# Banded attention in items of two query blocks, in a one-core two-model transformer kernel

## The reference, cut to what matters

```python
    kb = band(k).astype(jnp.float32)          # block b of 128 queries sees the keys of blocks b-1 and b
    vb = band(v).astype(jnp.float32)
    s = jnp.einsum('bnjqhgd,bnjkhd->bnjhgqk', qb, kb) * scale
    ...
    s = jnp.where(mask[:, None, None, :, :], s, jnp.float32(NEG))
    m = jnp.max(s, axis=-1, keepdims=True)
    if sinks is not None:
        sk = sinks.astype(jnp.float32).reshape(Hkv, G)[:, :, None, None]
        m = jnp.maximum(m, sk)
        p = jnp.exp(s - m)
        denom = jnp.sum(p, axis=-1, keepdims=True) + jnp.exp(sk - m)
    ...
    o = jnp.einsum('bnjhgqk,bnjkhd->bnjqhgd', p / denom, vb)
```

## Time and profile before

| | us |
|---|---|
| median of 3 runs | 2407.29 |
| lowest, highest | 2406.37, 2409.31 |
| span of the profiled execution | 2406.4 |

### The profile page before, as it was taken

One profiled execution on the slowest core, in us unless ns is written; L12 is line 12 of the kernel. 1 busy time (PEld: TensorE's weight loads), 2 busy tenths in 40 slices (PEclk: granted clock), 3 DMA queues, 4 the chain that ended last, 5 costly groups with the idle time before them and its releaser, 6 DMA issues.

```text
span 2406.4 us, 29717 instructions
## 1 busy us (share of the span) xinstructions
PE 2379.8 (99%) x11108; PEld 1924.6 (80%) x11108; DVE 1209.2 (50%) x1961; ACT 965.8 (40%) x1513; POOL 1316.2 (55%) x1589
## 2 busy tenths in 40 slices
PE   8999999999999999999999999999999999999999
PEld 8777778888888888777787888888887777788887
DVE  5997765423224432379625743333325785266331
ACT  4554444322223223566524432332336764344321
POOL 5763246656556655366244765555554562466554
PEclk9999999999999999999999999999999999999999
DMA  5321123333333333222122333333332221223333
GB/s 166 109 71 53 47 77 97 96 97 97 97 97 110 97 97 103 71 72 69 54 87 79 97 97 97 96 97 97 97 98 67 72 78 53 88 87 98 96 97 96
DMA packets 59758, 213.40 MB, mean 89 GB/s; under 512 B 6624, under 2 KB 6752, under 8 KB 59488
## 3 DMA queue, kind: packets, MB, share of 16 engines
q1 hardware_dynamic: 59472, 211.38, 29.2%
q10 hardware_dynamic: 144, 0.14, 0.0%
HBM read 209.39 MB, written 2.10 MB: 88 GB/s over the span
## 4 chain that ended last, share of the span: by engine, by line
PE 91%; DVE 6%; issue 1%; ACT 1%; DMA 0%; POOL 0%; SPq 0%; DVEq 0%; ACTq 0%
PE banks L721 89%; DVE t L1203 1%; DVE t L1211 1%; DVE t L1213 1%; DVE t L1488 1%; DVE t L1204 1%; DVE t L1197 1%; DVE t L1219 0%; PE banks L841 0%; PE banks L995 0%; DVE t L1222 0%; ACT t L1679 0%; DMA t<-in_w 0%; PE banks L875 0%; POOL t L1992 0%
## 5 line engine op out<-in xcount | busy, mean ns | idle before, releaser
L721 PE MATMUL banks<-t,t 128*128 128x512 f32 (+4 forms) x10788 | 2351.7, 387 | 17.2 <-ACT t L1699 5.9
L721 PEld LDWEIGHTS banks<-t,t 128*128 128x128 f32 (+2 forms) x10788 | 1889.5, 188 | 452.2 <-issue 64.3
L1992 POOL TENSOR_TENSOR t<-t,t 128x256 fp32r<-128x256 f32 x1544 | 1258.9, 846 | 1049.9 <-ACT t L1679 1041.5
L1679 ACT ACTIVATE t<-t 128x1024 fp32r<-128x1024 f32 x385 | 408.2, 1060 | 1078.8 <-issue 605.5
L1197 DVE TENSOR_TENSOR t<-banks,t 128x512 f32<-128x512 f32 x121 | 83.1, 687 | 169.8 <-PE banks L721 169.2
L1378 DVE TENSOR_TENSOR t<-banks,t 128x512 f32<-128x512 f32 x44 | 30.4, 690 | 184.5 <-PE banks L721 184.3
L1346 DVE SCALAR_TENSOR_TENSOR t<-banks,t 128x512 f32<-128x512 f32 x32 | 22.1, 691 | 155.4 <-PE banks L721 155.4
L1080 DVE SCALAR_TENSOR_TENSOR t<-t,t,t 128x512 fp32r<-128x512 f32 x64 | 52.0, 817 | 58.1 <-ACT t L1699 58.1
L1323 DVE TENSOR_TENSOR t<-t,t 128x512 fp32r<-128x512 f32 x68 | 70.5, 1036 | 2.3
L1352 DVE TENSOR_TENSOR t<-banks,t 128x512 f32<-128x512 f32 x24 | 16.6, 691 | 106.0 <-PE banks L721 106.0
L1699 ACT ACTIVATE t<-t,t 128x512 fp32r<-128x512 f32 x64 | 45.6, 715 | 55.7 <-DVE t L1346 49.1
(11 more groups left out here) (182 smaller groups left out, 1304.7 us busy)
## 6 DMA issues: line engine op xcount, KB each, us to landing
t<-in_w SPq DMA_DIRECT2D x386, 512.0 KB, 3.5
t<-in_xT SPq DMA_DIRECT2D x8, 256.0 KB, 5.7
out<-t SPq DMA_DIRECT2D x8, 256.0 KB, 4.5
t<-in_dmask SPq DMA_DIRECT2D x1, 1536.0 KB, 7.7
t<-in_vbias SPq DMA_DIRECT2D x2, 384.0 KB, 4.1
t<-in_c SPq DMA_DIRECT2D x1, 576.0 KB, 8.6
t<-in_w SPq DMA_DIRECT2D x2, 256.0 KB, 3.9
t<-in_pos SPq DMA_DIRECT2D x2, 256.0 KB, 4.1
```

What stands on the lines that cost most here:

```text
L721: return pe.matmul(o, l, r, start=start, stop=stop, skip_group_check=True)
L1679: a.activation(whl[u % 2][:, 0:1024], wraw[u % 3][:, :], ACT.Copy).then_inc(*w_high.next(u))
L1992: p.tensor_tensor(hl[:, 1024:2048][:, c], wraw[u % 3][:, c], as_f32(hl[:, c]), ALU.subtract).then_inc(*w_low.next((u, q)))
```

## The change

An item (i, c) now takes query blocks 2c and 2c+1, so there are 8 items in place of 16. Each score bank holds both blocks of one head (512 columns). The mask tile is three blocks wide (first, other, other) and one slice of 512 serves both c; a second small DMA fills its third part. Transposes go into the two score banks, and the turned probabilities are copied over the probabilities themselves in one 1024-wide tile (`swa_S`). The negated maximum with the sink is one DVE operation per head pair half (`tensor_scalar` with max and mult), and exp(sink - max) is formed on ACT with the sink as bias. There are 8 transposes and 8 value matmuls in an item. The planner's rules and its list of items behind the heads are the same, with one item still behind each group until the eight are used.

```diff
-        swm_t = at(top[0], 512)
+        swm_t = at(top[0], 768)
...
+        swa_S = [reg(88 + 6 * s, 1024)[:, :] for s in range(3)]
+        swa_m = [small_t[:, 64 + 16 * s:80 + 16 * s] for s in range(3)]
...
-            def swa_scores(i, b):
+            def swa_scores(i, c):
...
+                for q in range(2):
+                    b = 2 * c + q
+                    k0 = 128 * max(b - 1, 0)
+                    for hf in range(2):
+                        rows = slice(64 * hf, 64 * hf + 64)
+                        ins = mm(B[bk[hf]][:, 256 * q:256 * q + 256], QB[i][rows, 128 * b:128 * b + 128],
+                                 KBt[rows, k0:k0 + 256])
...
-                for k in range(4):
-                    ins = pe.transpose(B[bb][:, 128 * k:128 * k + 128], reg_S[slot][0][:, 128 * k:128 * k + 128], C["ident"])
...
+                for hf in range(2):
+                    for k in range(4):
+                        ins = pe.transpose(B[bk[hf]][:, 128 * k:128 * k + 128],
+                                           swa_S[slot][:, 512 * hf + 128 * k:512 * hf + 128 * k + 128], C["ident"])
...
+            def swa_soft(i, c):
...
                 for hf in range(2):
-                    v.scalar_tensor_tensor(out=sx[:, 256 * hf:256 * hf + 256], in0=B[pair(slot)[hf]][:, 0:256],
-                                           scalar=0.125, in1=mk, op0=M_, op1=A_).then_inc(*v_attn.next())
+                    v.scalar_tensor_tensor(out=sx[:, 512 * hf:512 * hf + 512], in0=B[pair(slot)[hf]], scalar=0.125,
+                                           in1=swm_t[:, 256 * c:256 * c + 512], op0=M_, op1=A_).then_inc(*v_attn.next())
...
-                v.tensor_tensor(m2[:, c0:c0 + 2], m2[:, c0:c0 + 2], sk, MX).then_inc(*v_attn.next())
...
-                v.tensor_scalar(m2[:, c0:c0 + 2], m2[:, c0:c0 + 2], -1.0, None, M_).then_inc(*v_attn.next(("swa_max", i, b)))
...
-                v.tensor_tensor(m2[:, c0 + 4:c0 + 6], m2[:, c0:c0 + 2], sk, A_).then_inc(*v_attn.next(("swa_sink", i, b)))
...
+                v.tensor_reduce(st_[:, 0:4], sx.rearrange("p (h k) -> p h k", h=4), AX, MX).then_inc(*v_attn.next())
...
+                    v.tensor_scalar(top_, top_, sink(i, hf), -1.0, MX, M_).then_inc(*v_attn.next(("swa_max", i, c)))
...
+                for k in range(4):
+                    part = sx[:, 256 * k:256 * k + 256]
+                    v.tensor_scalar(part, part, st_[:, 12 + k:13 + k], None, M_).then_inc(*v_attn.next(("swa_p", i, c)))
...
+                for hf in range(2):
+                    a.activation(st_[:, 8 + 2 * hf:10 + 2 * hf], st_[:, 2 * hf:2 * hf + 2], ACT.Exp,
+                                 bias=sink(i, hf)).then_inc(*a_attn.next())
...
-                sp.dma_start(swm_t[:, :], smask).then_inc(*in_swm.next("swm"))
+                sp.dma_start(swm_t[:, 0:512], smask).then_inc(*in_swm.next())
+                sp.dma_start(swm_t[:, 512:768], smask[:, 256:512]).then_inc(*in_swm.next("swm"))
...
-        banded = [swa_item(i, b) for b in range(4) for i in range(4)]
+        banded = [swa_item(i, c) for c in range(2) for i in range(4)]
```

More of the change, by code:

```diff
@@ L857, in dil_values @@
                 bank[bb] = [(v_attn, ("dil_pt1", t, r))]
-            def swa_scores(i, b):
-                ba, bb = pair(swa_at[i, b][0])
-                k0 = 128 * max(b - 1, 0)
+            def swa_scores(i, c):
+                bk = pair(swa_at[i, c][0])
                 need.wait_ge(*p_attn.at(("head", ("qb", i))))
                 need.wait_ge(*p_attn.at(("head", ("kb", 0))))
-                free(ba, bb)
-                for hf in range(2):
-                    rows = slice(64 * hf, 64 * hf + 64)
-                    ins = mm(B[(ba, bb)[hf]][:, 0:256], QB[i][rows, 128 * b:128 * b + 128], KBt[rows, k0:k0 + 256])
-                ins.then_inc(*t_attn.next(("swa_scores", i, b)))
@@ L870, in swa_turn @@
-            def swa_turn(i, b):
-                slot = swa_at[i, b][0]
-                bb = pair(slot)[1]
-                need.wait_ge(*v_attn.at(("swa_p", i, b)))
-                for k in range(4):
-                    ins = pe.transpose(B[bb][:, 128 * k:128 * k + 128], reg_S[slot][0][:, 128 * k:128 * k + 128], C["ident"])
-                ins.then_inc(*t_attn.next(("swa_turn", i, b)))
-                bank[bb] = [(a_attn, ("swa_pt", i, b))]
-            def swa_values(i, b):
-                slot = swa_at[i, b][0]
+                free(*bk)
@@ L889, in swa_values @@
-                ins.then_inc(*t_attn.next(("swa_values", i, b)))
-                bank[ba] = [(v_attn, ("swa_out", i, b))]
+                for q in range(2):
+                    k0 = max(2 * c + q - 1, 0)
+                    for k in range(2):
+                        for hf in range(2):
+                            o = 512 * hf + 256 * q + 128 * k
+                            ins = mm(B[ba][64 * hf:64 * hf + 64, 128 * q:128 * q + 128],
+                                     VB[:, k0 + k, 64 * hf:64 * hf + 64], swa_S[slot][:, o:o + 128], k == 0, k == 1)
@@ L892, in sb_scores @@
+                ins.then_inc(*t_attn.next(("swa_values", i, c)))
+                bank[ba] = [(v_attn, ("swa_out", i, c))]
             def sb_scores(l, t, p):
@@ L1302, in swa_norm @@
                 need.wait_ge(*v_attn.last())
                 for hf in range(2):
[L1304 to L1311 removed]
+                    top_ = st_[:, 2 * hf:2 * hf + 2]
@@ new lines, in swa_soft, with swa_norm @@
+                    v.tensor_scalar(top_, top_, sink(i, hf), -1.0, MX, M_).then_inc(*v_attn.next(("swa_max", i, c)))
+            def swa_norm(i, c):
+                slot = swa_at[i, c][0]
+                sx, st_ = swa_S[slot], swa_m[slot]
+                need.wait_ge(*a_attn.at(("swa_exp", i, c)))
+                v.tensor_tensor(st_[:, 4:8], st_[:, 4:8], st_[:, 8:12], A_).then_inc(*v_attn.next())
+                need.wait_ge(*v_attn.last())
+                v.reciprocal(st_[:, 12:16], st_[:, 4:8]).then_inc(*v_attn.next())
+                need.wait_ge(*v_attn.last())
+                for k in range(4):
+                    part = sx[:, 256 * k:256 * k + 256]
+                    v.tensor_scalar(part, part, st_[:, 12 + k:13 + k], None, M_).then_inc(*v_attn.next(("swa_p", i, c)))
@@ L1313, in halves1, with swa_out @@
+            def swa_out(i, c):
+                need.wait_ge(*t_attn.at(("swa_values", i, c)))
+                v.tensor_copy(OB[i][:, 256 * c:256 * c + 256],
+                              B[pair(swa_at[i, c][0])[0]][:, 0:256]).then_inc(*v_attn.next(("swa_out", i, c)))
             def halves1():
```

104 lines of the change are left out of this document (44 added, 60 removed).

## The result

| | before | after |
|---|---|---|
| median of 5 runs, us | 2407.85 | 2417.05 |
| lowest, highest | 2406.37, 2409.31 | 2414.18, 2417.84 |
| ratio, 95% interval | | 1.0034, 1.0023 to 1.0045 |
| span of the profiled execution | 2406.4 | 2415.2 (its run took 2417.05) |
| mean granted clock of PE in the runs | 0.998 (33 runs beside E1) | 0.996 |

What follows compares the result with a forecast made beforehand. It took PE as the bound (busy 99%), DVE as good as full beside the heads. Terms +8.8 - 3.8 - 1.2 - 2.0 = +1.8 on span 2406.4 gave 2408.2, plus 0.9 to the median: 2409.1 us, range 2401 to 2415.5.

Steps and rivals of the forecast that it cites:

- wait for the division, third to fifth item: PE's transposes would wait 8.8 us for the division, once or in pieces at the third to fifth item.
- waits of before that go: PE's old waits fall away: 3.8 us beside the heads (L1219, L1749, L1305) and 1.2 us at the end.
- PE's own work: Joined score and value steps of the eight items save between nothing and 4.8 us of PE; 2 us taken.
- no price here changes with it: PE's granted clock is 1.00 in all three windows read, so no price in the forecast changes with the clock.
- no PE wait from 210 to 330 us above 1 us: Sign that the forecast is right: behind the heads, no PE wait above 1 us in the new profile.
- Where it lands: Step placing the cost at the fifth item's turning: division ends at 186.3 us, PE comes at 177.5, waits 8.8.
- PE's own arrival: PE comes to the fifth item's transposes, at dense matmul 414, at 177.5 us, against 172.3 before.
- The divisions: DVE's four divisions of a double item priced at 0.703 us each, 14.1 us for the term of 20.
- the longer item holds up PE: Rival: one double item's latency in the full stretch makes PE wait 14.7 us; 2414.9 us, chance 0.16.
- The relief rival: Divisions mostly find the port free (0.353 us), PE waits 1.8 us; 2402.1 us, or 2399.3; chance 0.15.
- The weights' rival: ACT, held by DVE's lag, delays weight copies, so PE waits for low halves; +5, 2414 us, chance 0.07.
- the 337: Sign that the forecast is wrong: a last gate before 325 us or behind 337 us.

Runs made afterwards that it cites:

- E1: Changed kernel with a banded double item appended only behind the six ka head groups, order otherwise planned as before; 2403.01 us, ratio 0.9980.
- E7: Changed kernel with ten useless matmuls on PE ahead of the division wait of the third, fourth, fifth and seventh item; 2412.84 us, ratio 1.0023.
- E9: Changed kernel, same order, the four divisions still four operations but as tensor_tensor in place of tensor_scalar; 2420.40 us, ratio 1.0055.
- E2: Changed kernel with the planned time of each banded turning step (transposes) put 3 us later; 2412.12 us, ratio 1.0017.
- E4: Changed kernel, same order, the four divisions of 256 columns as one DVE operation of 1024 columns; 2406.79 us, ratio 0.9996.
- E12: Changed kernel with the planner's cost of one 256-column division at 0.83 us in place of 0.29, order planned anew; 2415.41 us, ratio 1.0040.
- E5: Changed kernel with double items only behind the six ka head groups and one division of 1024 columns per item; 2399.12 us, ratio 0.9969.
- E10: Kernel before, sixteen single items, with items only behind the six ka head groups and one division of 512 columns each; 2417.41 us, ratio 1.0042.

## Why the prediction was wrong, point by point

**The sum, term by term.** Forecast on the span +1.8, measured +8.8.

| term | forecast | measured |
|---|---|---|
| wait for the division, third to fifth item | +8.8 | +8.95 (2.90 + 3.21 + 2.84) |
| wait for the division in the gates | 0 | +2.60 |
| waits of before that go | -5.0 | -6.6 (2.1 + 1.9 + 1.4 + 1.2 in 58 to 335 us) |
| other waits | 0 | +1.3 (0.9 + 0.4) |
| clock in the stage | 0 | +3.4 |
| ahead of the stage (kb done at 59.8 us, not 58.6) | 0 | +1.2 |
| PE's own work | -2.0 | -2.0 (what is left over) |

The last row is no measurement of its own: the forecast's 2.0 is neither shown nor refuted by it. The forecast's last step, from the span to the median, was off as well. It added 0.9 us to the span of 2406.4, but the five runs of the kernel after took 1.8 to 1.9 us more than their spans (2417.05 and 2415.2), so the profiled run of before was a slightly long one, of about 2408.3. This costs the forecast about half a microsecond.

**"no price here changes with it"** is the step that failed most: the clock was put at nothing and took 3.4 us in the stage. The forecast took the clock as 1.00 because it was 1.00 in the kernel before, whose waits in the stage were 1.5 us at most, and priced a wait at its own length. E7 shows the rest: the same waits filled with useless work lose 4.2 us less. The Trainium skill (TensorE: Matmul & The Clock Gate, "What's actually happening") has the clock tied to PE's activity; the runs here agree, with a fall behind two of the four waits of the kernel after, at all four of E9 (3.1 to 3.7 us), none in E7, and one of 10.2 us that begins inside E2's wait of 7 us. The length of a single wait doesn't decide it, though: E4 has a fall behind a wait of 2.03 us, E1 none behind one of 2.63 us. Ahead of the stage there is one more fall, at 41.6 us, in code that the change doesn't touch; it cost 1.7 us, and PE waited 1.1 us less for POOL there (0.2 against 1.3), so the row in the table is a difference and not the price of a fall (the rest of it wasn't traced). Nine of the twelve experiments' profiles have a fall at that place and the profile of before has not; whether it has to do with the change isn't shown. So the share of the clock in the gap of the medians (9.2 us) is better read from the mean clocks of the runs: some 4 us (9.7 against 5.1 to 5.9), and the other 5 are waits less saved work.

**"no PE wait from 210 to 330 us above 1 us"** was wrong by 2.6 us at 256 us. The forecast took the division at its later median, 0.353, and DVE's 40 us to spare as a cover. At 256 us POOL was busy, the four divisions took 2.8 us, and ahead of them DVE, in order, had waited 1.86 us for a bank (the row of L1210 below); the item's last exponential had ended at 253.3 us, 1.4 us before that wait did. Spare time in a window's mean doesn't cover one item.

```profile
254.77 0.69 DVE L1210 TENSOR_TENSOR t<-banks,t 128x512 f32<-128x512 f32 x1 [1.86 <-PE banks L727]
255.37 0.46 DVE L1306 TENSOR_TENSOR t<-t 128x4 f32<-128x4 f32 x1
255.86 0.18 DVE L1308 RECIPROCAL t<-t 128x4 f32<-128x4 f32 x1
256.08 2.76 DVE L1312 TENSOR_SCALAR t<-t,t 128x256 f32<-128x256 f32 x4
```

**"Where it lands"** had the right size, 8.8 against 8.95 us, by a wrong road, which is luck. It counted DVE's queue as if it were never idle, one lag that grows to the fifth item. DVE was in fact busy 88% of 58.6 to 201.1 us, not over 94%, and from 90 to 214 us it sat 8.9 us before L1210 waiting for PE's banks (1.9 us in the kernel before, 90 to 205 us):

```profile
L1210 DVE TENSOR_TENSOR t<-banks,t 128x512 f32<-128x512 f32 x14 | 9.6, 687 | 8.9 <-PE banks L727 8.9
```

PE waited for DVE at an item, and DVE for PE behind it. PE's own arrival was right: 177.5 us plus what it had lost before (2.90 + 3.21 in the two waits, 1.7 by the clock, 1.2 ahead of the stage) is 186.5, and it came at 186.7 (189.54 - 2.84). Some of that is luck: the small waits that came new up to there (1.3 us) nearly cancel those of before that went (1.7 us), and the forecast counted neither. The divisions ended at 189.5 instead of 186.3.

**The divisions**, four at 0.703, were right as a mean (0.721) and wrong where it counted: four in a row took 1.1 us where POOL leaves room, 2.8 to 3.3 where it doesn't, and PE waits only for the second kind. E4 shows the price: one instruction in their place takes 10 us off, some 4 of them by the clock (9.7 against 5.9). The order is made with 4 x 0.29 us for them (0.155 + 256 x 0.00053 in the planner's costs), so by the plan the transposes of the slow items stand 1.6 to 2.2 us too early. That alone isn't the cause, though: E12 moved them and took 2415.4. By the Trainium skill (SBUF — State Buffer, "SBUF: two separate sides") POOL's operation and a DVE operation that is in a two-port mode or reads two SBUF tensors lock each other out for a whole instruction; E9's two-tensor form (0.94 beside POOL) agrees with it, and that rule taken at its word would have refused E9's theory.

**The rival "the longer item holds up PE"** was the right case, given 0.16. It had 2414.9, with the divisions at 0.808, a maximum of 1.37 (it took 1.22) and 1 us of ACT per item (DVE waited 1.2 us for L1810 in all six together). Its time was off by 2 us, and that by luck: its added terms weren't what the runs showed, and the clock and the gates, which it left out as the forecast did, made up for them. The relief rival is refuted here (waits of 11.5 us, not 1.8); its short waits come in E4 and E5 (2.4 and 1.0 us), a time below that of the kernel before only in E5. The weights' rival gave 0.9 us (L2002), not 5. The rest was as foretold: the mask operation 0.679 us, the bank behind head seventeen emptied at 214.2 (211 forecast), the last gate's bank emptied at 340.7 us (PE had ended it at 339.0), behind the 337 that the forecast named as the sign of its failure.

**Left open.** The interplay between heads and double items was shown by moving it (E2, E12) and relieving it (E1), not taken apart by engine. How much of E5's 8 us is the doubling isn't settled, since E10 crowds the gates and the single items that match E5's load, two behind each ka group, were not run. What decides whether the lower clock follows a wait of 2 to 3 us is open too.

## What to carry to other kernels

An item that is made twice as long costs through its longest chain at the place where it stands, not through its total; price its short operations in the contended state, count instructions rather than columns where POOL streams beside DVE, and join them into one. A larger item needs its places in the schedule thinned out as well: the same doubling went from 1.0034 to 0.9969 with half as many items beside the heads and one division. A new stall of PE of 2 us or more may cost more than its own length (here 1.7 us for each fall behind it, at a wait of 2.03 us as at one of 3.2 us), so give it a term for the clock and a wider range; a fill of useless matmuls is a quick test of that.

## What the runs showed of the hardware that was not expected

- Behind waits of 3.2 and 2.6 us PE was granted the lower clock for 3.4 us (cost 1.7 us), from within a wait of 7 us for 10.2 us (E2; E12 likewise); behind 2.9 and 2.84 us it wasn't in that profile, nor behind 2.63 us in E1, but it was behind 2.03 us in E4. Forty useless matmuls in the waits (9.2 us by the expectation's 0.23 us each) made the kernel 4.2 us faster (E7).
- A DVE operation of 256 columns costs 0.35 us alone, 0.81 beside POOL's 256-column stream and up to 1.37 beside POOL's 512-column one; four in a row pay four times (1.1 us from start to end without POOL, 2.8 to 3.3 beside it), one of 1024 columns once (1.22 and at most 1.51).
- Turning a scalar operation into one with two tensors doesn't free it from this (0.42 alone, 0.94 and up to 1.49 beside POOL).
